# First HGRN head of a two-branch encoder layer: gates of its first chunk computed apart, later chunks behind the queries, and the first output's rsqrt moved into POOL's key work

## What is computed

```
f  = lb + (1 - lb) * sigmoid(f_b)          # forget gate, 128 x 1152 of a head
k  = 1 - f
S_t = diag(f_t) S_{t-1} + k_t v_t^T        # per frame
o_t = S_t^T q_t                            # then RMS-normalised per head and gated by silu(g_b)
```

## Time and profile before

| | before |
|---|---|
| three timed runs | 2416.2, 2416.68, 2418.96 us (median 2416.68) |
| the profiled execution: its time, its span | 2416.9 us, 2414.4 us |
| PE busy | 2390.8 us (99% of the span) |
| DVE, ACT, POOL busy | 1280.2, 750.0, 487.9 us |
| mean granted TensorE clock | 0.999 |

### The profile page before, as it was taken

How to read it: one execution, slowest core, us unless ns; L and a number is a source line. 1 busy time by engine, 2 the same in 40 slices (tenths; PEclk the granted TensorE clock), 3 DMA queues, 4 the chain that set the end, 5 groups by cost and what they waited for, 6 DMA issues and landing times.

```text
span 2414.4 us, 36796 instructions
## 1 busy us (share of the span) xinstructions
PE 2390.8 (99%) x13984; PEld 2267.8 (94%) x13984; DVE 1280.2 (53%) x2404; ACT 750.0 (31%) x1454; POOL 487.9 (20%) x730
## 2 busy tenths in 40 slices
PE   8999999999999999999999999999999999999999
PEld 8999999999989999999999999889899899898896
DVE  4153525243376667667765444544655645646638
ACT  4133332323222222232222332324233233332334
POOL 1021202111165456536544000001000000000001
PEclk9999999999999999999999999999999999999999
DMA  5252725354424323432432634223102101101104
GB/s 176 93 193 68 244 71 189 125 180 128 137 87 139 124 85 114 142 107 95 139 131 84 225 115 152 98 88 97 53 18 70 44 25 64 49 26 61 41 24 161
DMA packets 219213, 257.25 MB, mean 107 GB/s; under 512 B 8164, under 2 KB 186728, under 8 KB 218984
## 3 DMA queue, kind: packets, MB, share of 16 engines
q1 hardware_dynamic: 219112, 255.89, 31.8%
HBM read 175.64 MB, written 80.22 MB: 106 GB/s over the span
## 4 chain that ended last, share of the span: by engine, by line
PE 75%; issue 11%; DVE 7%; POOL 3%; DMA 2%; ACT 1%; SPq 1%; POOLq 0%; DVEq 0%; ACTq 0%
PE bank L627 11%; PE bank L628 11%; PE bank L629 11%; PE bank L902 6%; PE bank L903 6%; PE bank L904 6%; PE bank L951 5%; PE bank L952 5%; PE bank L950 5%; PE bank L818 1%; PE bank L931 1%; PE bank L930 1%; PE bank L932 1%; DMA ZQ<-scratch_z 1%; POOL ORS L1862 1%
## 5 line engine op out<-in xcount | busy, mean ns | idle before, releaser
L627 PE MATMUL bank<-XH,WHI 128*128 128x384 f32 x2256 | 769.9, 341 | 0.9 <-issue 0.6
L629 PE MATMUL bank<-XH,WLO 128*128 128x384 f32 x2256 | 755.1, 335 | 0.0
L628 PE MATMUL bank<-XL,WHI 128*128 128x384 f32 x2256 | 754.8, 335 | 0.0
L627 PEld LDWEIGHTS bank<-XH,WHI 128*128 128x128 f32 x2256 | 424.2, 188 | 5.4 <-issue 3.2
L628 PEld LDWEIGHTS bank<-XL,WHI 128*128 128x128 f32 x2256 | 424.3, 188 | 0.8
L629 PEld LDWEIGHTS bank<-XH,WLO 128*128 128x128 f32 x2256 | 423.8, 188 | 0.0
L1363 DVE TENSOR_TENSOR WLO<-WRAW,WHI 128x1024 fp32r<-128x1024 f32 x128 | 159.9, 1249 | 241.9 <-ACT WHI L1021 237.6
L1021 ACT ACTIVATE ZST<-bank 128x384 f32<-128x384 f32 x240 | 117.3, 490 | 526.6 <-PE bank L629 517.6
L902 PE MATMUL bank<-XH,WHI 128*128 128x384 f32 x768 | 256.8, 334 | 1.6 <-ACT XH L1021 1.6
L904 PE MATMUL bank<-XH,WLO 128*128 128x384 f32 x768 | 256.7, 334 | 0.0
L903 PE MATMUL bank<-XL,WHI 128*128 128x384 f32 x768 | 256.6, 334 | 0.0
(11 more groups left out here) (221 smaller groups left out, 3487.6 us busy)
## 6 DMA issues: line engine op xcount, KB each, us to landing
scratch_z<-ZST SPq DMA_DIRECT2D x80, 576.0 KB, 3.1
WRAW<-in_w_in SPq DMA_DIRECT2D x80, 512.0 KB, 3.9
HZ<-scratch_z SPq DMA_DIRECT2D x32, 576.0 KB, 5.2
WRAW<-in_w_up SPq DMA_DIRECT2D x32, 512.0 KB, 4.2
WDR<-in_w_down SPq DMA_DIRECT2D x32, 512.0 KB, 5.4
MG<-scratch_z SPq DMA_DIRECT2D x16, 576.0 KB, 5.5
ZQ<-scratch_z SPq DMA_DIRECT2D x4, 1152.0 KB, 6.6
ZK<-scratch_z SPq DMA_DIRECT2D x4, 1152.0 KB, 8.7
```

The costliest lines, as they stand in the source:

```text
L627: pe.matmul(psum[c][:, 0:CH], WHI[p][:, k, :], XH[:, k, s], start=(k == 0), stop=False)
L628: pe.matmul(psum[c][:, 0:CH], WHI[p][:, k, :], XL[:, k, s], start=False, stop=False)
L629: last = pe.matmul(psum[c][:, 0:CH], WLO[p][:, k, :], XH[:, k, s], start=False, stop=(k == KT - 1))
```

## The change

Only the order and the grain of work move; the same values are computed.

1. Ahead of the loops, ACT's sigmoid of the first head is split in columns 0 to 383 and 384 to 1151, and DVE's `forget(0)` likewise. DVE does the first piece, then the first part of the queries of chunk 0, then `wlo_block(41)`, the second part of the queries, and then the second piece of the gates. Before, `wlo_block(41)` and the whole of `forget(0)` stood ahead of the queries.
2. POOL clears RR of the first chunk before it waits, starts the keys of chunk 0 when the first piece is there, and waits for the second piece behind them.
3. In every head, DVE's `wlo_block` of slots 3, 6, 9 and 12 stands behind `prep_q` and `weights` of its slot.
4. In every head, POOL's `head_rs` of tile 0 moves from behind the two gates into `prep_k(h, 1)`, behind level 5: level 6, KRH, `H.k_ok` and the gates come after it.
5. TensorE's wait for the gates at the first tile (`H.fk`) is taken out (the waits for keys and queries stay), and the counts of the semaphores are raised by one.

```diff
@@ ACT
+            def forget_first():
+                act.wait_ge(H.in_[1], 16)
+                act.activation(FG[:, 0:CH], HZ[1][:, 0:CH], ACT.Sigmoid).then_inc(H.f_ok, 1)
+                act.activation(FG[:, CH:], HZ[1][:, CH:], ACT.Sigmoid).then_inc(H.f_ok, 1)
...
-            forget(0)
+            forget_first()
@@ DVE, inside a head's slots
-                        if c == 0 and jj:
-                            wlo_block(n + 1, (jj + 1) % 2)
                         if s in (1, 6, 7):
                             if s == 6:
                                 dve.wait_ge(H.sc, 9 * h + 3)
                             prep_q(h, 1 + s // 6, 0 if s < 7 else 1)
                         if s >= HA and s - HA < NT:
                             weights(h, s - HA)
+                        if c == 0 and jj:
+                            wlo_block(n + 1, (jj + 1) % 2)
@@ DVE, ahead of the loops
+            def forget_first(s, ready):
+
+                dve.wait_ge(H.f_ok, ready)
+                ch(dve.tensor_scalar(FG[:, s], FG[:, s], LBC[:, 1, 0:1], LBC[:, 0, 0:1], ALU.mult, ALU.add))
+                ch(dve.tensor_scalar(KK[:, s], FG[:, s], -1.0, 1.0, ALU.mult, ALU.add))
+                dve.sem_inc(H.fk, 1)
+
             ret_done(dve)
+            forget_first(slice(0, CH), 1)
+            dve.wait_ge(H.in_[0], 16)
+            prep_q(0, 0, 0)
             wlo_block(41, 1)
-            forget(0)
-            prep_q(0, 0, 0)
             prep_q(0, 0, 1)
+            forget_first(slice(CH, T), 2)
@@ POOL
             def hg_head(h, last):
-                prep_k(h, 1)
+                prep_k(h, 1, {5: 0})
                 for c in range(2):
                     gate(H, h, c, 1, HZ[3][:, c * CH:(c + 1) * CH].unsqueeze(1))
-                head_rs(H, h, 0)
                 head_rs(H, h, 1)
...
+            ch(pool.memset(RR[:, 0:CH], 1.0))
             pool.wait_ge(H.fk, 1)
-            prep_k(0, 0)
+            prep_k(0, 0, fresh=False)
+            pool.wait_ge(H.fk, 2)
```

More of the change, by code:

```diff
@@ L800, in hg_a @@
                     pe.wait_ge(H.in_[2], 16 * h + 16)
-                    pe.wait_ge(H.fk, h + 1)
                     pe.wait_ge(H.kz8, 2 * h + 1)
@@ L1574, in forget @@
             def forget(h):
-                dve.wait_ge(H.f_ok, h + 1)
+                dve.wait_ge(H.f_ok, h + 2)
                 ch(dve.tensor_scalar(FG[:, :], FG[:, :], LBC[:, 1, bass.ds(h, 1)], LBC[:, 0, bass.ds(h, 1)],
@@ L1907, in _, with prep_k @@
             ch.reset()
-            def prep_k(h, c, after={}):
+            def prep_k(h, c, after={}, fresh=True):
                 s = slice(c * CH, (c + 1) * CH)
@@ L1913, in prep_k @@
                 pool.tensor_tensor(FT[:, 0:CH // 2], FG[:, c * CH:(c + 1) * CH:2], FG[:, c * CH + 1:(c + 1) * CH:2], ALU.mult)
-                ch(pool.memset(RR[:, s], 1.0))
+                if fresh:
+                    ch(pool.memset(RR[:, s], 1.0))
                 for l in range(LEV):
@@ L1957, in hg_head @@
                 if not last:
-                    pool.wait_ge(H.fk, h + 2)
+                    pool.wait_ge(H.fk, h + 3)
                     pool.wait_ge(H.att, 9 * h + 10)
```

## The result

The changed kernel takes 2422.28 us (median of 20 runs, 2420.09 to 2423.6), the kernel before 2417.39 us beside it (median of 20 runs). The ratio is 1.002, with a 95% interval of 1.0014 to 1.0026: slower by 4.9 us, where +5.1 was forecast. The profiled execution took 2422.75 us, its span is 2420.9 us.

The account below looks back on a forecast made before the run. TensorE, busy 99% of the span, was taken as the bound. 8.9 us lost in heads two to eight less 3.75 gained in the first made +5.1 on 2416.9, so 2422.0, about 2421.8 by medians; range 2419 to 2425, wider 2412 to 2428.

Parts of the forecast that it names:

- Tile 0 at 671.7, no wait for POOL: First head, L809: POOL's keys end earlier, so the wait goes down to a few tenths, 3.2 us gained there.
- A new wait for the weights at tile 1: First head, L809: TensorE waits 1.7 us for DVE, tile 1 at 679.15, leaving 1.45 of the 3.2 gained.
- Part 4 ends the wait at L779 in the first head: First output's transpose: scaled output is there before TensorE comes, so the 2.2 us wait goes.
- With that the slow clock goes too: First head: half clock ends with the L779 stall; stall and slow clock together were put at 3.7 us.
- New waits of about 1 us at L809 and at L779 in each head: Heads after the first: TensorE waits about 1 us each for ATT at L809 and OT at L779.
- 1.4 us per head from the pairing: DVE's chunk-1 queries beside POOL's level 6, KRH and gates: stretch 6.4 instead of 5.0, tiles 1 to 5 27.4.
- The full exclusion: Rival: DVE stands still for all three POOL instructions, 2.07 us a head, 2427 in all; chance 0.12.
- the small price: Rival: only 0.4 to 1.0 us a head comes through, result 2415.5 to 2419.5; chance 0.22.
- The second to eighth head lose 8.9 together: Heads two to seven lose 1.4 us each, 8.4, and the eighth 0.5.
- The other parts: Parts 3 and 5, the moved WLO and dropped fk wait: zero, with 0.3 either way for part 3.
- the eighth head was to lose only 0.5: Last head: DVE ended 0.9 us before TensorE came, so that slack leaves a loss of 0.5.
- The sum: Whole kernel: 8.9 us lost, 3.75 gained in the first head, +5.1, so 2422.0; chance 0.50.

Follow-up runs that it names:

- where the longest wait was 0.88: Kernel with the power between KRH and the gates, plus the first head's second piece of gates made by ACT instead of DVE: 2410.19 us, 0.9973 of before.
- the kernels that take the pairing away: Two, on the changed kernel: tile 0's rsqrt back behind the gates, 2412.64 us; rsqrt behind KRH and ahead of the gates, 2411.63 us.
- the one that adds only reads: Kernel before with four extra POOL products per head behind tile 0's rsqrt, reading SBUF and writing scratch: 2423.78 us, 1.0028 of before.
- part 4 alone: Kernel before with only tile 0's rsqrt moved into the keys of chunk 1, behind level 5: 2429.16 us, 1.0049 of before.
- parts 1 and 2 alone: Kernel before with the first head's split sigmoid and gates, queries between; WLO of the slots and rsqrt in their old places: 2415.52 us, 0.9994 of before.
- part 3 alone: Kernel before with only WLO of slots 3, 6, 9 and 12 moved behind queries and weights: 2415.05 us, 0.9992 of before.
- the writes: Kernel before with four extra POOL clears of 384 columns per head behind tile 0's rsqrt, writing SBUF only: 2416.15 us, 0.9997 of before.

## Why the forecast was right, and where it was not

The direction, its cause and the total were right; that the total came so close is partly luck. Point by point:

- **Tile 0 at 671.7, no wait for POOL:** it came at 671.75 with 0.24 of idling.
- **A new wait for the weights at tile 1, 1.7 us, tile 1 at 679.15:** the mechanism was right, the term too small: 2.80 and 680.48. DVE's path from HZ[0]'s landing to the weights was put at 19.9 us and took 21.1 (659.20 to 680.33). The two instructions of the gates (0.68 and 0.56) had been priced at 1.2 without the gaps around them; from the end of QP at 671.38 to the next PP at 673.20 it is 1.82. The queries of chunk 0 with WLO took 12.2 instead of 11.7, and the rest 7.1 instead of 7.0 (16.4 and 1.1 less the 10.5). These three make 1.2 of the 1.3; the other 0.1 is the start at 659.20 instead of 659.1. DVE by time in the changed kernel:

```profile
671.53 0.68 DVE L1653 TENSOR_SCALAR HZ<-HZ,LBC 128x768 f32<-128x768 f32 x1 [0.16 <-DVE QP L1553]
672.24 0.56 DVE L1654 TENSOR_SCALAR KK<-HZ 128x768 f32<-128x768 f32 x1
673.20 1.04 DVE L1535 COPY PP<-HZ 128x384 f32<-128x384 f32 x1 [0.39 <-DVE KK L1654]
```

- **Part 4 ends the wait at L779 in the first head:** the wait is gone, but not through part 4. With part 4 taken back out it is gone as well (longest wait 0.2), since the earlier start brings the output forward by 2.06. So part 4 gave nothing for its price.
- **"With that the slow clock goes too":** this step was wrong. I had put the slow clock down to the second stall at L779 and removed it with that stall. The runs show it behind other long waits too: behind 2.80 here, and in no place of the stage only where the longest wait was 0.88. It cost 1.66 in the first head. With the 1.3 of the line on tile 1 this makes 3.0, of which 0.6 came back, since the rest of tiles 1 to 5 took 26.8 and not 27.4. So tile 5 came only 1.4 earlier (710.30 to 708.91) and not 3.75.
- **New waits of about 1 us at L809 and at L779 in each head:** those at L779 came, somewhat smaller (0.65 in the second head, 0.80 in the eighth); those at L809 hardly (0.2 at most). The loss comes through the scaled output, not through the weights.
- **1.4 us per head from the pairing of POOL's level 6 and KRH with DVE's queries:** DVE's stretch grew by 1.41, and the kernels that take the pairing away (5.11 and 5.00) and the one that adds only reads (6.09) show it as the cause. On TensorE it comes to 1.3 a head when the rest of the change is in (9.3 over heads two to eight, from -1.5 without part 4 to 7.8 with it). The full exclusion (2.07) and the small price both fall.
- **The second to eighth head lose 8.9 together:** by the distances from tile 0 to tile 0, and from tile 0 to tile 8 in the last head, they lost 7.8: 1.20, 0.79, 1.26, 0.94, 1.23, 1.17 and 1.21. Two terms were off. Heads two to seven were put at 8.4 and lost 6.6. The other parts were priced at nothing in these heads, but the loss is smaller with them (0.79 to 1.26 a head) than with part 4 alone (1.33 to 1.55), by 0.3. That part 3 does this is likely but not shown alone: it gives 0.2 a head by itself, and parts 1 and 2 by themselves, which touch nothing in these heads, 0.1. And the eighth head was to lose only 0.5, because the weights of tile 4 had 0.9 in hand; it lost 1.2. I had read the slack at the wrong reader. TensorE was not stopped there by the weights of tile 4 but by the scaled output of tile 2, whose mean comes on DVE behind the weights of tile 3 and behind WLO. DVE and TensorE by time, eighth head of the changed kernel:

```profile
1299.01 1.22 DVE L1367 TENSOR_TENSOR WLO<-WRAW,WHI 128x1024 fp32r<-128x1024 f32 x1
...
1300.60 0.15 DVE L1443 TENSOR_SCALAR OMS<-OSS 128x1 f32<-128x1 f32 x1
...
1302.14 0.33 PE L779 MATMUL bank<-ident,OT 128*128 128x128 f32 x1 [0.80 <-ACT OT L1127]
```

- **The sum:** in these two executions TensorE reaches tile 0 of the first head at the same moment but for its wait (671.64 and 671.51), so their times up to the second head can be compared directly: its tile 0 starts at 761.52 instead of 762.73, a gain of 1.2. Behind it 7.8 are lost. That makes 6.6 by the profiles; the spans differ by 6.5, the medians by 4.9 (3.4 to 6.3 by the interval). The forecast had 8.9 and 3.75. The missing gain of 2.5 and the smaller loss of 1.1 leave 1.4 between forecast and profiles, and the medians happen to lie on the other side, so the closeness of +5.1 to +4.9 is partly luck.

What the parts are worth by medians, each kernel against the kernel before beside it: part 4 costs 9.1 on top of the others and 12.3 alone; parts 1 to 3 gain 4.2 together; parts 1 and 2 alone show 1.2 and part 3 alone 1.8, neither told from nothing. In the first head parts 1 and 2 need part 3, since it takes WLO out of the way of the weights that the earlier start makes urgent (a wait of 4.19 without it, 2.36 with it). Why part 4 alone costs more than on top of the others stays open. In the profiles it doesn't: from tile 0 of the first head to tile 8 of the last it costs 10.9 alone and 11.0 on top. The kernel with part 4 alone has five runs, of which one took 2425.54 and four 2428.85 to 2429.51.

## What to carry over

Before an instruction that waits for another engine is moved up in a queue, see what lands behind it and on which work of the awaited engine it falls: here the wait was for a value that DVE makes right before its own critical stretch, so three POOL instructions moved from a free place into it. Put such a wait behind the work that nobody hinders; this one step turned a kernel 4.9 us slower into one 5.2 us faster. And when one wait is removed at the start of a stage, follow the second-latest input to the next tile before the gain is counted, since it may be given back there with interest.

## What the hardware showed that I had not expected

**Half clock followed waits of two to four microseconds, but not each.** In the first head the granted clock fell to 0.50 (1.2 GHz) for some 3.4 or 6.8 us around TensorE's waits of 2.36, 2.80 and 4.19 for the weights of tile 0, and not around the one of 0.88. In the kernel before it fell for some 3.4 us around the 2.22 at L779. As a price: 1.6 to 1.7 us on top of a wait of 2.4 to 2.8, and 2.4 on top of the 4.19. But the wait alone doesn't decide it. The 3.2 ahead of tile 0 in the kernel before brought none directly (5.76 to the next tile), while the same wait brought 3.4 us of it in the kernel with part 3 alone (7.36) and some 6.8 us in the ones with part 4 alone (8.41), with the reads (8.80) and with the writes (8.82), and up to this point the code on TensorE is the same in all of these. With one profiled execution of each, it can't be told whether the kernels differ here or only the executions. What decides it, these runs don't settle, so no price of the first head that rests on one profile is sure to better than 2 or 3 us.

**POOL's reads and DVE's chain.** Level 6 and KRH (2.07 us before, 2.36 in their new place) in five microseconds of DVE steps cost DVE 1.41, spread over three steps: 0.41, 0.19 and 0.80. The 2.46 us of four shorter reads cost 1.09, spread over four steps, each 0.20 to 0.33 longer. Single steps show the pattern plainly: PP takes 0.35 undisturbed and 1.15 beside KRH.
